# Background work in pieces of half the size, in a two-layer diffusion backbone with an expert search

## What is computed

```python
def expert_block(xb):                                   # 128 tokens
    q = (xb @ p['peer_wq']).reshape(PEER_CHUNK, PEER_HEADS, 2, PEER_KEY_HALF)
    s = jnp.einsum('thcd,ckd->thck', q, p['peer_subkeys'])
    sv, si = lax.top_k(s, PEER_TOPK)                     # 16 of 128, for both halves
    cand_s = sv[:, :, 0, :, None] + sv[:, :, 1, None, :] # 256 sums
    top_s, pos = lax.top_k(cand_s, PEER_TOPK)
    eidx = jnp.take_along_axis(cand_i, pos, axis=-1)     # 128 experts for each token
    gate = jax.nn.softmax(top_s, axis=-1)
    u, v = peer_u[eidx], peer_v[eidx]
    act = jax.nn.gelu(jnp.einsum('ted,td->te', u, xb), approximate=False) * gate
    return jnp.einsum('te,ted->td', act, v)
```

## Time and profile before

| | |
|---|---|
| median of 3 runs | 2668.57 us |
| profiled execution | 2667.46 us, its span 2665.3 us |
| PE busy | 2085.1 us (78%) |
| DVE busy | 1850.8 us (69%) |
| ACT busy | 1150.3 us (43%) |
| POOL busy | 958.5 us (36%) |
| DMA | 969.74 MB, 364 GB/s over the span |
| mean granted clock of PE | 0.902 |

### The profile page before, as it was taken

How to read it: one execution, slowest core, us unless ns; L and a number is a source line. 1 busy time by engine, 2 the same in 40 slices (tenths; PEclk the granted TensorE clock), 3 DMA queues, 4 the chain that set the end, 5 groups by cost and what they waited for, 6 DMA issues and landing times.

```text
span 2665.3 us, 25899 instructions
## 1 busy us (share of the span) xinstructions
PE 2085.1 (78%) x6680; PEld 1069.7 (40%) x6680; DVE 1850.8 (69%) x4482; ACT 1150.3 (43%) x3035; POOL 958.5 (36%) x916
## 2 busy tenths in 40 slices
PE   6997778879898888777677978769877887667775
PEld 2455434534454445333323333334543444333322
DVE  0146976975678769988876656554588686877775
ACT  2123483462377644434454333432245664433332
POOL 1012243333333333444445444430133433345542
PEclk9998899889899999888988998889888998899888
DMA  8479989989898899999999999996499999999997
GB/s 336 128 270 350 389 322 373 395 314 391 326 392 317 307 385 352 364 417 420 405 422 396 420 419 416 405 390 240 165 413 380 415 365 390 416 384 420 421 407 317
DMA packets 206904, 969.74 MB, mean 364 GB/s; under 512 B 17308, under 2 KB 69048, under 8 KB 108472
## 3 DMA queue, kind: packets, MB, share of 16 engines
q0 software_dynamic: 123648, 855.69, 79.6%
q1 hardware_dynamic: 83128, 112.56, 12.3%
HBM read 967.14 MB, written 1.05 MB: 363 GB/s over the span
## 4 chain that ended last, share of the span: by engine, by line
PE 34%; DVE 24%; DMA 21%; ACT 12%; issue 7%; POOL 1%; SPq 0%; POOLq 0%; DVEq 0%; ACTq 0%
DMA EXPERT<-in_peer_uv,FIX 20%; PE VS L964 14%; PE PA L824 10%; DVE EXPERT L1574 8%; DVE ACC L1584 2%; PE PA L852 2%; DVE SCR L1200 2%; PE PB L954 2%; ACT L1148 1%; ACT L1096 1%; PE PB L892 1%; ACT WEI L1150 1%; PE VS L782 1%; ACT DIAG L1155 1%; ACT HT L1053 1%
## 5 line engine op out<-in xcount | busy, mean ns | idle before, releaser
L964 PE MATMUL VS<-EXPERT,DIAG 128*128 128x512 f32 x2304 | 1205.0, 666 | 303.0 <-ACT DIAG L1155 302.5
L659 POOL DMA_INDIRECT EXPERT<-in_peer_uv,FIX x768 | 887.8, 1156 | 1163.7 <-PE VS L964 770.9
L1574 DVE CUSTOM_DVE_ANT_0 EXPERT<-EXPERT,H 128x1024 f32<-128x1024 f32 x768 | 924.2, 1223 | 324.6 <-DMA EXPERT<-in_peer_uv,FIX 314.3
L964 PEld LDWEIGHTS VS<-EXPERT,DIAG 128*128 128x128 f32 x2304 | 466.0, 213 | 908.9 <-issue 485.1
L1148 ACT ACTIVATE GEL<-DOT 128x1 f32<-128x1 f32 x768 | 155.2, 202 | 1024.2 <-DVE DOT L1574 1023.4
L824 PE MATMUL PA<-WT,HT 128*128 128x512 f32 (+2 forms) x720 | 298.5, 562 | 17.1 <-ACT HT L1053 7.8
L1584 DVE SCALAR_TENSOR_TENSOR ACC<-EXPERT,WEI,ACC 128x1024 f32<-128x1024 f32 x192 | 246.0, 1281 | 38.6 <-ACT WEI L1150 38.6
L1155 ACT ACTIVATE DIAG<-IDN,WEI 128x128 f32<-128x128 f32 x576 | 231.3, 401 | 71.3 <-PE VS L964 53.7
L1150 ACT ACTIVATE WEI<-GEL,GATE 128x1 f32<-128x1 f32 x768 | 226.3, 295 | 25.0
L954 PE MATMUL PB<-HT,WT 128*128 128x128 f32 (+1 forms) x1280 | 204.4, 321 | 17.2 <-issue 14.5
L954 PEld LDWEIGHTS PB<-HT,WT 128*128 128x128 f32 x1280 | 191.6, 215 | 44.8 <-issue 35.1
(11 more groups left out here) (146 smaller groups left out, 1681.7 us busy)
## 6 DMA issues: line engine op xcount, KB each, us to landing
EXPERT<-in_w_ada POOLq DMA_DIRECT2D x48, 1024.0 KB, 13.2
WT<-in_peer_wq SPq DMA_DIRECT2D x80, 512.0 KB, 14.9
WT<-in_w_in SPq DMA_DIRECT2D x48, 512.0 KB, 10.4
WT<-in_w_out SPq DMA_DIRECT2D x40, 512.0 KB, 8.6
EXPERT<-in_peer_uv,FIX POOLq DMA_INDIRECT x768, 11.4
WT<-in_w_in SPq DMA_DIRECT2D x16, 384.0 KB, 10.3
WT<-in_w_in SPq DMA_DIRECT2D x16, 288.0 KB, 5.9
WT<-in_mla_wq_up SPq DMA_DIRECT2D x4, 512.0 KB, 8.7
```

Source lines behind the costliest of these rows:

```text
L659: pool.indirect_dma_start(out=EXPERT[:, j, :], out_offset=None, in_=a["peer_uv"], in_offset=bass.IndirectOffsetOnAxis(ap=FIX[:, par, j:j + ...
L964: ins = nc.tensor.matmul(VSUM[n][:, :], DIAG[:, i, :], EXPERT[:, j, D + n * W:D + (n + 1) * W], start=first, stop=last_one)
L1574: nc.vector.tensor_tensor_reduce(out=EXPERT[:, j, 0:D], in0=EXPERT[:, j, 0:D], in1=H2[:, b % HB, :], scale=1.0, scalar=0.0, op0=ALU.mult, ...
```

## The change

Five edits, with the same arithmetic and the same transfers:
1. `in` and `out` have one weight row per part instead of two; `up` is cut into single rows too. The weights still come in pieces of two rows.
2. For projections of several tiles, DVE takes the first tile at the last row, and the others in a stage of its own, `land`.
3. A head of the search has four stages instead of two. PE: the keys' matmuls and half of the first query, its other half, half of the second query, its other half. DVE: the top sixteen of both halves, the best sums, the comparison, the indices. ACT copies the first query at the second stage and the second one at the fourth.
4. The costs are changed to fit (`in` 20 to 2 x 8 and 15 for `land`).
5. In the opening the vectors 2 to 5 of layer 0 are spread over the projections and most of the attention; vector 0 of layer 1 stands before `heads`, vector 1 before the second norm. Nothing of the conditioning is left behind the first head. POOL's wait for the output weights is gone.

```diff
@@ front, attention ... pick
         out += [("in", l, g, n, ts, part) for part in range(PARTS)]
+        if len(ts) > 1:
+            out.append(("land", l, g, n, ts))
...
     for h in range(PH + 1):
-        out += [("pick", l, g, h, ts), ("more", l, g, h, ts)]
+        out += [(kind, l, g, h, ts) for kind in HEAD]
         if h > 0 and len(ts) > 1:
-            out += [("also", l, g, h, ts[1:]), ("then", l, g, h, ts[1:])]
+            out += [(kind, l, g, h, ts[1:]) for kind in ALSO]
@@ holds
-    return s[0] in ("in", "out") and s[-1] < PARTS - 1
+    return (s[0] in ("in", "out") and s[-1] < PARTS - 1 or s[0] == "in" and len(s[4]) > 1
+            or s[0] == "up" and s[-1] < UPS[s[3]][1] - 1)
@@ COST
-COST = {... "in": (0, 20), ... "up": (0, 25), ... "out": (0, 22), "pick": (45, 0), "more": (40, 0), "also": (45, 0), "then": (40, 0),
+COST = {... "in": (0, 8), "land": (15, 0), ... "up": (0, 9), ... "out": (0, 11), "pick": (23, 0), "rank": (25, 0),
+        "more": (15, 0), "lift": (22, 0), "also": (23, 0), "rank too": (25, 0), "more too": (15, 0), "lift too": (22, 0),
@@ make_plan
-    plan += mingle(attend[:-2], modulation(0, (2, 3, 4))) + [("mod", 0, 2)]
-    plan += attend[-2:-1] + products(0, 5) + [("adae", 0, 5)] + attend[-1:] + [("adat", 0, 5)]
-    plan += leave[:-2] + products(1, 0) + [("adae", 1, 0), leave[-2], ("adat", 1, 0)] + products(1, 1)[:1] + first[:4]
-    plan += products(1, 1)[1:] + [("adae", 1, 1), ("adat", 1, 1), ("mod", 1, 1), leave[-1]]
+    plan = plan[:-len(start[4:])] + mingle(start[4:] + attend[:-2], modulation(0, (2, 3, 4, 5))) + [("mod", 0, 2)]
+    plan += attend[-2:-1] + products(1, 0) + [("adae", 1, 0)] + attend[-1:] + [("adat", 1, 0)]
+    plan += leave[:-2] + products(1, 1) + [("adae", 1, 1), leave[-2], ("adat", 1, 1), ("mod", 1, 1)] + first[:TWO] + leave[-1:]
@@ gpsimd, staged
-                    if ADAS[m] == ("ada", 1, 0, SPAN - 1):
-                        pool.wait_ge(piece_used, OUT_ISSUED)
@@ tensor, key_query
-            def key_query(stage, c):
+            def key_query(stage, c, part):
                 _, l, g, h, ts = stage
                 mine = slice(ts[0] * P, (ts[-1] + 1) * P)
-                bank = fill_b()
-                for k in range(KD):
+                if part == 0:
+                    held["query"] = fill_b()
+                for k in range(part * HP, part * HP + HP):
...
-                last.then_inc(filled_b, 1)
-                held[h, c] = rb.n
+                if part == 1:
+                    last.then_inc(filled_b, 1)
+                    held[h, c] = rb.n
@@ vector, in_
-                for t in ts:
+                landed_tiles(stage, ts[:1])
+
+            def land(stage):
+                landed_tiles(stage, stage[4][1:])
```

More of the change, by code:

```diff
@@ L42 @@
 SPAN = KD // KP
+HEAD = ("pick", "rank", "more", "lift")
+ALSO = ("also", "rank too", "more too", "lift too")
 RING = 8
@@ L102, in front, with upward @@
     if keys:
-        out += [("up", l, g, "v", ts), ("turn", l, g, "k", ts)]
+        out += upward(l, g, "v", ts) + [("turn", l, g, "k", ts)]
     return out
+def upward(l, g, what, ts):
+    return [("up", l, g, what, ts, part) for part in range(UPS[what][1])]
 def attention(l, g, t):
@@ L157, in splits_pick @@
 def splits_pick(s):
-    return s[0] in ("pick", "more") and s[3] > 0 and len(s[4]) > 1
+    return s[0] in HEAD and s[3] > 0 and len(s[4]) > 1
 def mingle(first, second):
@@ L175, in mingle @@
     return out + second[at:]
-COST = {"stat": (45, 0), "norm": (50, 0), "in": (0, 20), "turn": (0, 10), "root": (5, 5), "up": (0, 25), "attn": (35, 0),
-        "hnorm": (20, 0), "heads": (20, 0), "gates": (10, 0), "out": (0, 22), "back": (20, 0), "pick": (45, 0), "more": (40, 0), "also": (45, 0), "then": (40, 0),
+COST = {"stat": (45, 0), "norm": (50, 0), "in": (0, 8), "land": (15, 0), "turn": (0, 10), "root": (5, 5), "up": (0, 9), "attn": (35, 0),
+        "hnorm": (20, 0), "heads": (20, 0), "gates": (10, 0), "out": (0, 11), "back": (20, 0), "pick": (23, 0), "rank": (25, 0),
+        "more": (15, 0), "lift": (22, 0), "also": (23, 0), "rank too": (25, 0), "more too": (15, 0), "lift too": (22, 0),
         "ada": (18, 0), "adae": (4, 0), "adat": (10, 0), "mod": (5, 0)}
@@ L191, in picks_of @@
 def picks_of(stage):
-    if stage[0] not in ("more", "then") or stage[3] == 0:
+    if stage[0] not in ("lift", "lift too") or stage[3] == 0:
         return []
@@ L1124, in more, with lift @@
                     gate_exps(ts[0])
+            def lift(stage):
                 key_query(stage, 1)
@@ L1133, in key_query, with more_too @@
                         .then_inc(emptied_b, 1)
-            def then(stage):
+            def more_too(stage):
                 gate_exps(stage[4][0])
@@ L1175, in _ @@
             do = {"consts": consts, "tables": tables, "adae": adae, "stat": stat, "norm": norm, "root": root, "turn": turn, "attn": attn,
-                  "hnorm": hnorm, "heads": heads, "pick": pick_, "more": more, "then": then, "slots": slots,
+                  "hnorm": hnorm, "heads": heads, "rank": rank, "more": more, "lift": lift, "more too": more_too, "slots": slots,
                   "last": last_}
@@ L1306, in in_, with landed_tiles @@
                     dve.wait_ge(filled_b, turned[pend_free[what]])
-                for t in ts:
+                landed_tiles(stage, ts[:1])
+            def land(stage):
+                landed_tiles(stage, stage[4][1:])
+            def landed_tiles(stage, some):
+                _, l, g, what, ts = stage[:5]
+                for t in some:
                     bank = from_a()
@@ L1366, in up @@
             def up(stage):
-                _, l, g, what, ts = stage
+                _, l, g, what, ts, k = stage
+                if k < UPS[what][1] - 1:
+                    return
                 if what in ("q", "k", "v"):
@@ L1486, in pick_, with rank, lift @@
                 top(ts[0])
+            def rank(stage):
+                if stage[3] > 0:
+                    best(stage[4][0])
             def more(stage):
+                if stage[3] > 0:
+                    compare()
+            def lift(stage):
                 _, l, g, h, ts = stage
@@ L1494, in also @@
                 top(stage[4][0])
-            def then(stage):
-                _, l, g, h, ts = stage
-                experts(l, g, h - 1, ts[0])
             def mark(ins):
@@ L1640, in _ @@
                   "in": in_, "out": out_, "gates": gates, "up": up, "root": root, "turn": turn, "attn": attn,
-                  "hnorm": hnorm, "heads": heads, "pick": pick_, "more": more, "also": also, "then": then, "slots": slots,
-                  "close": close, "last": last_}
+                  "hnorm": hnorm, "heads": heads, "pick": pick_, "rank": rank, "more": more, "lift": lift, "also": also,
+                  "rank too": rank, "more too": more, "lift too": lift, "land": land, "slots": slots, "close": close, "last": last_}
             for stage in late(PLAN):
```

120 lines of the change are left out of this document (68 added, 52 removed).

## The result

The changed kernel takes 2690.23 us, the median of 4 runs (2688.13 to 2695.47); the kernel before took 2669.42 beside it (2667.14 to 2673.43). The ratio is 1.0079, with a 95% interval of 1.0060 to 1.0099: some 21 us slower, where I had forecast 9 us faster. The profiled execution took 2691.26 us (span 2689.3).

What follows compares the result with a forecast made beforehand. Gather transfers bind, except that PE binds layer 0's latent projections. The terms -0.7 - 2 + 1 - 8 + 1 = -8.7 us gave a median of 2659.9 us; the forecast's own range was 2653 to 2664, the whole range 2641 to 2677.

Steps and rivals of the forecast that it cites:

- opening: Conditioning moved ahead of the first head: -4.4 + 4.6 - 3.4 + 2.5 = -0.7 us, bounds -4 and +5.
- single rows: Layer 0's latent projections: pieces of one row followed by one slot save 3 us of PE's idle time.
- slots moved by the costs: Three slots leave layer 0's latent projections (-5) for stages that transfers bind (+7.7, or less): +1 us.
- landing apart: Layer 1's three-tile projections: PE waits 8 us for banks, once or twice, mostly covered by buffers: +1, bounds 0 and +8.
- heads in four, all searches: Long searches -8 us (bounds -18 and 0) from shorter DVE runs; one-tile searches +1 (bounds -6 and +20).
- about 5 us can be had: Layer 0's latent projections: of PE's 15 us idle, 8.8 stay where block 0 closes; 3 us were taken.
- 0.93: Sign for the projections: PE's busy share at 0.93 or more.
- wrong rival: Low clock after PE's holes at the heads, 1.7 us each; put inside rival 2, without a chance of its own.
- the buffers' cover: Three-tile projections of layer 1: eight gather buffers cover most of PE's 8 us bank wait, leaving +1 us.
- under 362 and 408: Sign for the two long searches: under 362 and 408 us for the same slots, DMA share 0.99 and over.
- under 80 us: One-tile searches: the sign was PE's waits before the keys' matmuls over 80 us in total instead of 62.6.
- Rival 2: Slower by PE's wait at the search heads, transfers running dry: about 2687 us, at half the price 2677; chance 0.19.

Runs made afterwards that it cites:

- heads in two: Changed kernel with no slot between a head's first and second or third and fourth stage, all else as changed: 2693.93 us, ratio 1.0080.
- inner rows: Kernel before with single rows only for each projection's first six rows: 2677.84 us, ratio 1.0023; with four-stage heads added: 2672.28 us, ratio 1.0007.
- the shifted one: Kernel before with one rounding in the weaver changed, so that many slots lie one stage earlier: 2682.69 us, ratio 1.0045.

## Why the prediction was wrong, step by step

| step | predicted, us (bounds) | alone, us (95%) |
|---|---|---|
| opening | -0.7 (-4 to +5) | +3.5 (0 to +7) |
| single rows | -3 of idle time | +23 (+17 to +29) |
| slots moved by the costs | +1 | +1 (-3 to +5) |
| landing apart | +1 (0 to +8) | +9 (+5 to +13) |
| heads in four, all searches | -7 | -7.5 (-11 to -4) |
| sum | -8.7 | +29; together measured +21 |

The measured values are the ratios of the single parts times 2672 us. They add up to 8 us more than the change as a whole, within what their intervals allow, and the parts needn't add: the new costs give the single rows another placement than the old ones, and the landing's wait is shorter between single rows.

1. **The step that failed is the rows'.** The prediction took PE's 15 us of idle time in the latent projections, saw that 8.8 of them stay at the block's end, and concluded that "about 5 us can be had". It read the holes that were there and never asked which hand-overs had no hole because a slot covered them. In the earlier trace rows the opening shows the bare hand-over of the transposed queries at 0.73 us; between slots the same hand-over also waits for a slot that ACT has ahead of the copy, for that slot's dot and for all that DVE has ahead of the dot, and that can be 4.88 us. In the changed kernel the two hand-overs of this stage stand at 2.20 and 6.09 us, where they stood at 0.73 and 0.25; in the run with the rows alone the stage took 16.4 us more, where the prediction had 3 less. PE was busy for 0.87 of the stage, not for the 0.93 that the prediction named as its sign. The bounds, -8 and +4, came from the same idle time, so they were too narrow as well.
2. **The clock stood in the wrong rival.** It priced the low clock at 1.7 us per hole for the heads and put it aside, since PE doesn't bind the searches. It does bind the latent projections, which the prediction itself had said, and 6.3 of the 16 us there are the clock. The rule of the Trainium skill that the prediction cited, "TensorE: Matmul & The Clock Gate", section "HAM oscillation — how this bites in real kernels", says that holes in PE's work throw the clock back to half. The rows of 3.68 us for 1.88 agree; I had applied it to the wrong stages.
3. **Landing**: the mechanism was right, and even its place (PE's row at slot 412, banks free behind DVE's slot 415). The wait too was priced rightly, at 8 us: in the changed kernel it is 7.96 us. What was mis-sized is the buffers' cover, which was to leave 1 us. In the changed kernel the same slots of that stage took 3.7 us longer in all, inside the bounds; alone, with rows in pairs and five slots between the landings, the wait was 13.38 us and the stage 10 us longer. While PE waits it frees no buffer (POOL's 17.39 us), so the buffers can't cover all of a wait of the engine that frees them.
4. **Heads**: alone, right in sign and size, and as far as one execution tells in place. In the changed kernel nothing of the gain shows: its long searches took 370.4 and 413.6 us for the slots that took 369.8 and 413.5 before (under 362 and 408 was the sign), and with heads in two it was no slower (1.0080 instead of 1.0079). Between inner rows they gave 4 us, with overlapping intervals. Why it doesn't show there was not tried. The wait before the keys' matmuls stayed under 80 us.
5. **Opening**: inside its bounds, at their upper half.
6. **None of the rivals was the right one.** Rival 2 ended on the slower side, by a mechanism that the traces don't bear out. Its range, 2677 to 2687, is below the result, as is the upper end of the whole range. Its sum has a slip: 24 - 6 + 2 is 20, not 18, which would make 2689; that this lies near the measured 2690 is luck. The rival that was missing is any order in which a slot stands on the wrong side of a transpose or a norm.
7. Attention's longer time was not foreseen. The last tile's took 82.9 us in the changed kernel and in each of its three variants with the same slot positions there, and 77.4 to 79.5 us in the kernels of the sets whose positions there are those of the kernel before, or all but one of them. The kernel before with the new totals alone has the changed kernel's positions and took 82.3 us. So it is placement too; which slot does it was not tried. The +1 of the costs in the table is therefore a balance of gains and losses.

## What to carry to other kernels

Where two streams are woven by a cost table, a change of grain is a change of placement, and placement has to be priced at the hand-overs: list each place where one engine waits for another's copy, and see in the order of every engine that no piece of the other stream stands ahead of that copy, and that one stands behind what it waits for. A rounding moved this kernel by 0.45%, a few units of cost and one rule for glued stages by about 0.2%, as much as the edits were to bring, so parts should be compared with all other slots held in place. And a stage whose engine binds got worse here by more than its holes.

## What the runs showed of the hardware

A hole of PE can have a second price here. Behind 4.88 us the next four records took 3.68 us instead of 1.88, behind 3.21 us also 3.68, and in the stage as a whole 421 records took 157.50 us instead of 151.25 for 422, at a granted clock of 0.91 instead of 0.95. These are the levels 1.2 and 2.4 GHz. Holes of 0.73 us didn't show it. Near 2 us the hole's length alone doesn't tell: behind 2.15 us in the kernel before twelve records took 5.42 us, and behind 2.16 us in the shifted one, with a hole of 1.97 us shortly ahead of it, 7.11.

Left open: in the changed kernel's second search PE stands idle ahead of query matmuls with no releaser in the profile,

```profile
488.85 2.05 PE L977 MATMUL PB<-HT,WT 128*128 128x128 f32 x8 [4.95 <-issue]
```

and over the span this wait comes to 22.0 us in 5 places (14.5 in 4 before). The weight pieces in `WT` that SP issues from 480 to 540 us take long to land (the smallest, median and largest):

```profile
DMA to landing us min/median/max: 13.1/15.7/24.9
```

In the kernel before they took 8.3, 13.8 and 18.5 us in the same window. That these pieces are what PE waits for, behind gathers in flight, is argued and not shown; no run tried it.
